# A three-part transformer kernel on one core: the differential bias is written a head ahead, latent outputs get a bank of their own, and neighbourhood heads run in pairs with their score products side by side

## The reference

```python
def diff_attention(q, k, v, lam, subln_w, lam_init):      # 8 heads, 2 maps of 64 each, v of 128
    def block(args):                                      # 16 meta queries, then 4 blocks of 128
        dist = (qpos[:, None] - kpos[None, :]).astype(jnp.float32)
        logits = (jnp.einsum('bhmqd,bhmkd->bhmqk', qblk, kt) * scale
                  - slopes[:, None, None, None] * dist)   # slope of the head: the bias
        probs = jax.nn.softmax(jnp.where(valid, logits, NEG_INF), axis=-1)
        attn = probs[:, :, 0] - lam * probs[:, :, 1]
        return jnp.einsum('bhqk,bhkv->bhqv', attn.astype(vt.dtype), vt)

def _neighbourhood_attention(q, k, v, k_ctx, v_ctx, rpb, n_rows):
    s_loc = jnp.einsum('bjqhd,bjakhd->bhjqak', q_r, k_b) + bias   # keys of the window, with bias
    s_ctx = jnp.einsum('bjqhd,bkhd->bhjqk', q_r, k_ctx)           # and 256 context keys
    p = jax.nn.softmax(jnp.concatenate([s_loc, s_ctx], axis=-1), axis=-1)
    o = einsum(p_loc, v_b) + einsum(p[..., n_loc:], v_ctx)

def _attend(q, k, v):                                     # latent attention: 768 keys, q of 96, v of 64
    s = jnp.einsum('bqhd,bkhd->bhqk', q * q.shape[-1] ** -0.5, k).astype(jnp.float32)
    p = jax.nn.softmax(s, axis=-1).astype(v.dtype)
    return jnp.einsum('bhqk,bkhd->bqhd', p, v)
```

## Time and profile before

| | us |
|---|---|
| median of 3 runs | 3075.2 (3074.88 to 3077.19) |
| the profiled execution's own time | 3074.74 |
| its span, first to last instruction | 3072.9 |
| TensorE busy | 2920.8 (95%) |
| VectorE busy | 1528.0 (50%) |
| ScalarE busy | 1144.4 (37%) |
| GpSimd busy | 35.1 (1%) |
| TensorE clock granted, mean | 0.969 |

### The profile page before, as it was taken

One profiled execution on the slowest core, in us unless ns is written; L12 is line 12 of the kernel. 1 busy time (PEld: TensorE's weight loads), 2 busy tenths in 40 slices (PEclk: granted clock), 3 DMA queues, 4 the chain that ended last, 5 costly groups with the idle time before them and its releaser, 6 DMA issues.

```text
span 3072.9 us, 42976 instructions
## 1 busy us (share of the span) xinstructions
PE 2920.8 (95%) x14922; PEld 2397.4 (78%) x14922; DVE 1528.0 (50%) x2441; ACT 1144.4 (37%) x1767; POOL 35.1 (1%) x28
## 2 busy tenths in 40 slices
PE   8999998899999999999999999889889899899998
PEld 6878777679987888879988888867656677788887
DVE  3335444455565666667744654655443434433334
ACT  4333355432223233255532423523444443432223
POOL 0000000000000000000000000000000000000000
PEclk9999999899999999999999999899889999899999
DMA  3224211143443554546643333311111113133332
GB/s 115 69 68 134 66 48 52 58 132 114 124 130 98 163 153 151 155 123 173 180 117 94 89 96 91 107 42 33 42 32 37 35 33 99 56 89 90 95 96 82
DMA packets 504093, 288.73 MB, mean 94 GB/s; under 512 B 17577, under 2 KB 483962, under 8 KB 503850
## 3 DMA queue, kind: packets, MB, share of 16 engines
q1 hardware_dynamic: 503978, 287.25, 31.9%
HBM read 285.12 MB, written 2.10 MB: 93 GB/s over the span
## 4 chain that ended last, share of the span: by engine, by line
PE 68%; issue 20%; DVE 5%; ACT 4%; DVEq 1%; ACTq 1%; DMA 0%; POOL 0%; POOLq 0%; SPq 0%
PE unit_acc L789 61%; DVE w_lo L2030 2%; PE aux L773 1%; PE aux L1340 1%; ACT w_hi L1439 1%; PE aux L1225 1%; PE aux L1316 1%; PE aux L916 1%; DVE mla_stat L2763 1%; PE aux L1207 1%; PE aux L810 1%; PE aux L1208 0%; ACT mla_p L1931 0%; DVE mla_pT L2769 0%; DVEq L2034 0%
## 5 line engine op out<-in xcount | busy, mean ns | idle before, releaser
L789 PE MATMUL unit_acc<-h_hi,w_hi 128*128 128x512 f32 (+1 forms) x2376 | 839.1, 377 | 21.7 <-DVE w_lo L2030 11.2
L789 PE MATMUL unit_acc<-h_lo,w_hi 128*128 128x512 f32 (+1 forms) x2376 | 816.7, 368 | 0.0
L789 PE MATMUL unit_acc<-h_hi,w_lo 128*128 128x512 f32 (+1 forms) x2376 | 815.2, 367 | 0.0
L2030 DVE TENSOR_TENSOR w_lo<-raw,w_hi 128x1024 fp32r<-128x1024 f32 (+3 forms) x418 | 496.6, 1188 | 578.5 <-ACT w_hi L1439 571.7
L1439 ACT ACTIVATE w_hi<-raw 128x1024 fp32r<-128x1024 f32 (+3 forms) x418 | 430.4, 1030 | 698.3 <-PE unit_acc L789 654.2
L789 PEld LDWEIGHTS unit_acc<-h_hi,w_hi 128*128 128x128 f32 x2376 | 431.5, 192 | 120.9 <-issue 21.4
L789 PEld LDWEIGHTS unit_acc<-h_hi,w_lo 128*128 128x128 f32 x2376 | 430.8, 191 | 78.3
L789 PEld LDWEIGHTS unit_acc<-h_lo,w_hi 128*128 128x128 f32 x2376 | 433.0, 192 | 72.1
L789 PE MATMUL unit_acc<-branch_hi,w_hi 128*128 128x512 f32 x448 | 178.3, 398 | 0.1
L789 PE MATMUL unit_acc<-branch_hi,w_lo 128*128 128x512 f32 x448 | 177.6, 397 | 0.0
L789 PE MATMUL unit_acc<-branch_lo,w_hi 128*128 128x512 f32 x448 | 177.6, 396 | 0.0
(11 more groups left out here) (368 smaller groups left out, 3696.1 us busy)
## 6 DMA issues: line engine op xcount, KB each, us to landing
raw<-in_ffn_w_dram SPq DMA_DIRECT2D x180, 512.0 KB, 3.8
raw<-in_w_in_dram SPq DMA_DIRECT2D x142, 512.0 KB, 3.9
ada_raw<-in_w_ada_dram SPq DMA_DIRECT2D x72, 512.0 KB, 4.7
raw<-in_w_up_dram SPq DMA_DIRECT2D x32, 512.0 KB, 4.2
raw<-in_w_down_dram SPq DMA_DIRECT2D x32, 512.0 KB, 3.9
raw<-in_w_branch_dram SPq DMA_DIRECT2D x24, 512.0 KB, 3.9
raw<-in_ffn_w_dram SPq DMA_DIRECT2D x24, 384.0 KB, 3.4
raw<-in_w_out_dram SPq DMA_DIRECT2D x16, 512.0 KB, 3.9
```

Of the source, the lines that this page charges most:

```text
L789: last = pe.matmul(G[s][0:n, 512 * j:512 * j + m], w[:, k, 0:n], x[:, k, a:a + m], start=(k == 0 and i == 0), stop=(k == kc - 1 and i == 2))
L2030: dve.tensor_tensor(wl[s][:, 0:kc, :], raw[s][:, 0:kc, :], wh[s][:, 0:kc, :].bitcast(F32), ALU.subtract).then_inc(lo_split, 1)
```

## The change

What it does, by place:

- The context's sum of squares stands after unit 7 of the feed-forward part, not after unit 6.
- Differential heads: ScalarE writes `diff_bias` for the next head after the last exponents of this one (`head_bias`), and for head 0 ahead of the loop. The filler is cut 4 and 4 chunks instead of 3 and 5, ScalarE copies the transposes of tile 4 before it takes the next head's projection, and VectorE's weight splits stand elsewhere.
- The start of the neighbourhood stage: splits stand between the three tables, and units 0 to 2 run one after another.
- Neighbourhood pairs: 4 steps, each of both heads. The four score products alternate between rows 0 to 63 and 64 to 127 of the array and write one bank for each head. Both heads share statistics instructions of two columns; one copy by ScalarE moves all eight transposes (VectorE's two copies before), ScalarE copies the values too, and the value products of both heads go to `NA_OUT`, a bank of `G[0]`.
- Latent heads: the value product goes to `MLA_OUT`, the second bank of one of the two accumulators, and waits for its own tile's copies alone; transposes no longer wait for the output before. Filler and splits are cut anew, a drain is added ahead of the reciprocal.

The diff, cut to what moves work:

```diff
+        NA_OUT = G[0][:, 512:512 + P]
+        MLA_OUT = G[Count(U_MLA).slot][:, 512:512 + VD]
...
                 qk(4)
-                fill(0, 0, 3)
+                fill(0, 0, 4)
                 qk(3)
...
-                fill(0, 3, 8)
+                fill(0, 4, 8)
...
-                    if final and n == 6:
+                    if final and n == 7:
                         sum_squares(ssc, GC)
...
+                def qk(t):
                     a = NA_START[t]
-                    pe.matmul(A[0][:, b:b + 256], q, nk[r, a:a + 256], start=True, stop=True)
-                    pe.matmul(A[0][:, b + 256:b + 512], q, kct[r, 2 * i + p, :], start=True, stop=True).then_inc(n_qk, 1)
+                    for b, k, k0 in ((0, nk, a), (256, kct[:, 2 * i + p, :], 0)):
+                        for e in range(2):
+                            r = slice(64 * e, 64 * e + 64)
+                            last = pe.matmul(A[0][:, 512 * e + b:512 * e + b + 256], nq[r, P * t:P * t + P],
+                                             k[r, k0:k0 + 256], start=True, stop=True)
+                    last.then_inc(n_qk, 1)
...
+                def pv(t):
+                    pe.wait_ge(n_at, val(at_(t + 1)))
+                    pe.wait_ge(n_o, val(at_(t) + 1))
...
-            for c in range(KC):
-                for k in range(2):
-                    unit(Count(U_NA + k), H2H, H2L, GS, ready=None if k else (ap_lo, 5 * KC),
-                         part=(c, c + 1))
-            unit(Count(U_NA + 2), H2H, H2L, GS)
+            for k in range(3):
+                unit(Count(U_NA + k), H2H, H2L, GS, ready=None if k else (ap_lo, 5 * KC))
...
                     if t:
                         pe.wait_ge(k_ad, val(cnt(t)))
                         pe.wait_ge(k_at, val(cnt(t)))
-                    if t > 1:
-                        pe.wait_ge(k_o, val(cnt(t - 1)))
...
-                    pe.wait_ge(k_ad, val(cnt(min(t + 2, NT))))
+                    pe.wait_ge(k_ad, val(cnt(t + 1)))
+                    if t:
+                        pe.wait_ge(k_o, val(cnt(t)))
                     for j in range(6):
-                        last = pe.matmul(A[1][:, 768:768 + VD], mT[t % 2][:, j, :], mV[:, j, :],
+                        last = pe.matmul(MLA_OUT, mT[t % 2][:, j, :], mV[:, j, :],
...
+            def head_bias(head):
+
+                act.activation(dR[:, :], rel[:, :], ACT.Copy,
+                               scale=cst("slope8")[:, bass.ds(head, 1)]).then_inc(d_bias, 1)
...
                 exps(3)
+                copy_pT(4)
                 next_head(0)
-                copy_pT(4)
                 exps(2)
                 out_o(4)
                 copy_pT(3)
                 exps(1)
+                if more:
+                    head_bias(head + 1)
                 out_o(3)
                 copy_pT(2)
...
+                    act.wait_ge(n_tr, val(turn(i, t + 1 + NT * p, 2 * NT)))
+                    act.activation(nT[:, :, :, :], A[1][:, :].rearrange("p (e c n) -> p e c n", e=2, n=P),
+                                   ACT.Copy).then_inc(n_at, 1)
...
                 for t in (4, 3, 2, 1):
                     logits(t)
+                    if t == 4:
+                        split(u + 4)
                     combine(t)
-                    if more and t == 3:
+                    if more and t == 2:
                         split(u + 5)
...
+                if kind < 2:
+                    split(Count(U_NA + kind + 2))
...
                 for t in range(NT):
                     if t < NT - 1:
                         row_max(t + 1)
+                    if more and t == 1:
+                        split(u + 2)
+                    if more and t == 2:
+                        split(u + 3, 4)
                     copy_pT(t)
                     if t:
                         out_o(t - 1)
-                    if more and t == 0:
-                        split(u + 2)
-                    if more and t == 1:
-                        split(u + 3, 4)
```

More of the change, by code:

```diff
@@ L1210, in transpose_p, with at_ @@
[L1210 to L1215, removed]
-                    last.then_inc(n_tr, 1)
[L1218 to L1222, removed]
-                    v0 = NA_START[t] // 64
-                    for j, v in enumerate((v0, v0 + 2, NV, NV + 1)):
-                        last = pe.matmul(A[1][:, 512:512 + NA_HD], nT[s % 2][:, j, :], nV[:, v, 64 * e:64 * e + 64],
-                                         start=(j == 0), stop=(j == 3))
+                def at_(t):
+                    return turn(i, t + NT * p, 2 * NT)
@@ new lines, in pv @@
+                def pv(t):
+                    pe.wait_ge(n_at, val(at_(t + 1)))
+                    pe.wait_ge(n_o, val(at_(t) + 1))
+                    v0 = NA_START[t] // 64
+                    for e in range(2):
+                        for j, v in enumerate((v0, v0 + 2, NV, NV + 1)):
+                            last = pe.matmul(NA_OUT[:, 64 * e:64 * e + 64], nT[:, e, j, :],
+                                             nV[:, v, 64 * e:64 * e + 64],
+                                             start=(e == 0 and j == 0), stop=(e == 1 and j == 3))
@@ L1599, in diff_head @@
                 head = i * 2 + e
-                act.drain()
-                act.activation(dR[:, :], rel[:, :], ACT.Copy,
-                               scale=cst("slope8")[:, bass.ds(head, 1)]).then_inc(d_bias, 1)
                 exps(4)
@@ L1627, in _ @@
             act.wait_ge(rel_in, 16)
+            head_bias(0)
             for k in range(3):
@@ L2317, in diff_head @@
                                          op1=ALU.subtract).then_inc(br_lo, 1)
-                if more:
-                    split(u + 7)
             dve.drain()
-            for k in range(3):
+            for k in range(2):
                 split(Count(U_DIFF + 2 + k))
@@ L2633, in _, with cnt, logits @@
                         [P, NA_H, 32, GRID_H]), ALU.add)
+                if kind < 2:
+                    split(Count(U_NA + kind + 2))
+            table.then_inc(n_tab, 1)
+            dve.memset(nst[:, :, :], 0.0)
             dve.drain()
-            dve.memset(nst[:, :, :], 0.0).then_inc(n_tab, 1)
-            dve.drain()
-            for k in range(3):
-                split(Count(U_NA + k + 2))
             def na_pair(i, p):
                 u = turn(i, U_NA + 3 * p, 6)
-                for half in range(2):
-                    dve.drain()
-                    dve.wait_ge(n_vt, val(turn(i, half + 1 + 2 * p, 4)))
-                    if half == 0:
-                        dve.tensor_copy(nV[:, 0:5, :], A[1][:, 0:640].rearrange("p (c n) -> p c n", n=P)).then_inc(
-                            n_v, 1)
-                    else:
-                        dve.tensor_copy(nV[:, 5:9, :], A[1][:, 0:512].rearrange("p (c n) -> p c n", n=P)).then_inc(
-                            n_v, 1)
-                def cnt(k):
-                    return turn(i, k + 8 * p, 16)
-                def logits(s):
-                    e, t = divmod(s, NT)
-                    b = s % 2
+                def cnt(t):
+                    return turn(i, t + NT * p, 2 * NT)
+                def logits(t):
                     kind = (0, 1, 1, 2)[t]
@@ L2689, in na_pair @@
-                logits(0)
-                logits(1)
-                for s in range(8):
-                    copy_pT(s)
-                    if s:
-                        out_o(s - 1)
-                    if s < 6:
-                        logits(s + 2)
-                    if s in (3, 6):
-                        split(u + 4 + s // 3)
-                out_o(7)
-                split(u + 7)
+                    dve.wait_ge(n_pv, val(cnt(t + 1)))
+                    at_ = i * 256 + 2 * p * NA_HD
@@ new lines, in out_o @@
+                    dve.tensor_tensor(nO[:, t, at_:at_ + P].rearrange("p (e n) -> p e n", e=2),
+                                      NA_OUT.rearrange("p (e n) -> p e n", e=2),
+                                      nst[:, 7, :].unsqueeze(2).to_broadcast([P, 2, NA_HD]), ALU.mult).then_inc(n_o, 1)
+                logits(0)
+                split(u + 4)
+                for t in range(NT):
+                    reciprocals(t)
+                    if t < NT - 1:
+                        logits(t + 1)
+                    out_o(t)
+                    if t == 1:
+                        split(u + 5)
@@ L2701, in na_pair @@
+                split(u + 6)
                 dve.drain()
@@ L2706, in _ @@
                     na_pair(i, p)
+            split(Count(U_LORA + 4))
             for c in range(4):
```

143 lines of the change are left out of this document (77 added, 66 removed).

## The result

The changed kernel takes 2971.1 us (median, 2969.6 to 2977.4) against 3076.2 for the one before in the same comparison: ratio 0.9661, 95% interval 0.9644 to 0.9678. That is 105 us less, where 90 were forecast. The part on the prediction says where the 15 us come from.

What follows compares the result with a forecast made beforehand. TensorE's own work and its gaps bound the kernel (busy 2920.8 of 3072.9 us). Gains 5.9 + 14.5 + 7.0 + 33.9 + 28.2 = 89.5 took 3074.7 to 2985.2, median 2986 us; 8-in-10 range 2970 to 3012.

Steps and rivals of the forecast that it cites:

- The sum of squares: Context's sum of squares behind unit 7: unit 7 fills the gap of a 4.58 us wait, gaining 5.9 us.
- Differential heads: Score product's 2.65 us wait goes, a new one of about 1.5 us comes at value product 2: 14.5 us gained.
- Start of the neighbourhood stage: Splits between the bias tables end TensorE's 5.17 us wait, a wait of some 0.2 stays: 7.0 us gained.
- Neighbourhood pairs: Eight score records in alternating halves take 1.25 us, idle and low clock shrink in four pairs: 33.9 us gained.
- Latent heads: Output in another bank ends the value product's wait; idle 21.5 to about 2, clock 10.7 to 2: 28.2 us.
- A: Neighbourhood pairs: halves don't overlap, or the chain is longer than the filler; 13.9 us more, 3000 us; chance 0.12.
- B: Pairs, latent and differential heads: the clock doesn't come back, 18 us likely not gained, 3004 us; chance 0.17.
- C: Latent and differential heads: waits only move, the 15.5 us turn up at the transposes, 3001 us; chance 0.13.
- D: Neighbourhood pairs: slower, the level stays at 1.2 GHz through all four, 3120 us; chance 0.03.

Runs made afterwards that it cites:

- the experiment on the bias: The changed kernel with the differential bias written in its own head again, ahead of the exponents of tile 4: 2979.1 us.
- the two kernels above: The kernel before with the latent heads' part alone, 3036.0 us, and the kernel before with the differential part alone, 3059.5 us.
- the kernel with the later bias: The changed kernel with the next head's differential bias written after the transposed copy of tile 1, not ahead of the output of tile 3: 2968.1 us.

## Why the prediction was right, and where it was off

The mechanisms came as written: the waits that were named went, and the new one came where it was expected. The gain came out larger than forecast in each stage, most of all in the latent heads. Heads are counted from 0 here.

*The sum of squares.* 5.9 forecast, 6.3 measured. The wait on the low weights before unit 7 and no wait at the sum, as worked out:

```profile
1293.38 0.50 PE L791 MATMUL unit_acc<-h_hi,w_hi 128*128 128x512 f32 x1 [0.94 <-DVE w_lo L2056]
1299.08 0.60 PE L803 MATMUL aux<-ctx_ssq,const 128*128 128x256 f32 x2
```

*Differential heads.* 14.5 forecast, 14.7 and 17.8 measured. In head 2, which starts at 401.39 here, against the earlier trace rows:

```profile
405.55 0.94 PE L954 MATMUL aux<-diff_k,diff_q 64*128 64x400 f32 x4
...
422.23 1.12 PE L981 MATMUL aux<-diff_v,diff_pT 128*128 128x128 f32 x6 [0.90 <-ACT diff_pT L1603]
```

The 2.65 us wait is gone and the new one is where the queue on ScalarE put it. It is 0.7 to 1.3 us, seven times, 6.8 in all, not 7 x 1.5 = 10.5. Against that, 4.9 us of the old waits stayed and not 2.2: 2.9 at the last head's score products and 2.0 at its value products, which the prediction didn't count. So 13.2 us of waits went where 12.2 were forecast. The clock over the stage rose from 0.93 to 0.94 and 0.95, some 3 and 6 us, where 2.3 were forecast. That the sum agrees with the first profile to 0.2 us is in part luck: errors of 3.7 and 2.7 us nearly cancel. The prediction also read head 2 as typical; as the experiment on the bias shows, the weight split was last in the others.

*Start of the neighbourhood stage.* 7.0 forecast, 8.0 measured; the two kernels above that leave this part as it was took 641.8 and 642.1 us here for 638.9, so the gain may be up to 3 us more. The 5.17 us wait is gone. What stayed is not 0.2: a wait of 2.3 us at the units in turn went (first row, kernel before) and one of 2.0, for another operand, came with the units one after another (second row, changed kernel).

```profile
1992.91 0.71 PE L789 MATMUL unit_acc<-h_hi,w_hi 128*128 128x512 f32 x1 [2.27 <-DVE w_lo L2030]
...
1976.22 0.51 PE L791 MATMUL unit_acc<-h_hi,w_hi 128*128 128x512 f32 x1 [2.01 <-DVE h_lo L2459]
```

The clock was 0.89 over the last 40.6 us ahead of the pairs and is 1.00 over the last 30.9.

*Neighbourhood pairs.* 33.9 forecast, 36.2 measured. A step, against the earlier trace rows:

```profile
2033.57 1.06 PE L775 MATMUL aux<-const,na_p 128*128 128x128 f32 x8 [0.76 <-ACT na_p L1894]
2034.57 0.70 PE L1206 MATMUL aux<-na_k,na_q 64*128 64x256 f32 x4
2035.10 0.60 PE L1206 MATMUL aux<-ctx_k,na_q 64*128 64x256 f32 x4
2035.63 0.50 PE L791 MATMUL unit_acc<-h_hi,w_hi 128*128 128x512 f32 x1
...
2037.14 1.89 PE L1225 MATMUL unit_acc<-na_v,na_pT 128*128 128x64 f32 x16
2040.33 1.04 PE L775 MATMUL aux<-const,na_p 128*128 128x128 f32 x8
```

Idle of 0.8 in a pair and 2.0 in the first came as written. Eight records took 1.06 (2034.57 to 2035.63), not 1.25: the Trainium skill's rule ("TensorE: Matmul & The Clock Gate", Part 3) was the better of the two values, by 3 us in the sum. Low clock cost 1.4 us, not 3.

*Latent heads.* 28.2 forecast, 33.6 and 35.2 measured; this is the term that was mis-sized. The prediction took "235.5 us of work" as busy time less slow clock, and let only the shown idle go. But busy time itself fell: 232.3 less 0.01 x 234 is 230.0. The 5.5 us between them are the part of a wait that the rows count as busy. The value product of tile 0 started 2.50 us after its transposes (2313.10 here, and 2315.60 in the earlier trace rows) where it now takes 0.66, so its wait cost 1.84, 0.16 more than the 1.68 shown. The next two rows are tile 1:

```profile
2313.10 0.82 PE L773 MATMUL aux<-const,mla_p 128*128 128x128 f32 x6
...
2322.03 0.82 PE L773 MATMUL aux<-const,mla_p 128*128 128x128 f32 x6
2323.02 1.52 PE L1340 MATMUL aux<-mla_v,mla_pT 128*128 128x64 f32 x12 [0.17 <-DVE mla_pT L2769]
```

It is 0.99 from start to start there, of which 0.17 is shown: again 0.16 more than shown. If the eight waits of the score product are like them, 32 waits in the stage make 5.1. The terms for idle (2) and clock (2) were right: 1.8, and 0.01 x 234 = 2.3.

*Rivals.* A (no overlap) is out: it took a chunk in between to bring it about. B (the clock doesn't come back) is out for the pairs, by 0.91 to 0.99, and for the latent heads, by 0.96 to 0.99, though pauses of 0.8 us stayed in three pairs; in the differential heads only a part came back. C (the waits only move) is out: the latent 15.5 us turned up nowhere, and the 6.8 at value product 2 are less than half of the 16.8 that the differential score product no longer waits. D is out.

The stages' gains add up to 98.8 us in the first profile and 103.7 in the second; less the 1.7 at the end that is 97 and 102, as the spans have it (97.3 and 102.5). The forecast of 89.5 is short of them by 8 and 13, and the latent heads alone make 5.4 and 7.0 of that. The 105 of the medians is 3 more than the second; the runs of the kernel before scatter by 7 to 14 us in each comparison of the experiments, and what of it is chance stays open.

## What to carry to other kernels

A wait cost more than its row showed here, as the products ahead of it no longer overlapped with the one behind: read the distance from start to start with and without the wait, in every head and not in one. When an instruction is moved off one chain, follow the queue that it now stands in: there it will be late next. A shorter chain can pay twice, since a slow clock can follow the pause: all four waits of 2.06 us in the pairs of the kernel before were followed by a low stretch in its profile. But compare low clock over several executions before counting it as a gain of an edit.

## What the runs showed of the hardware

- Two products of 64 rows in different halves of the array run at the same time even when they aren't neighbours in the program: 1.07 us for eight records in either order, 2 x 1.06 = 2.12 with three full-height products between them. With both products of one half first in the program, the first of the other half still started within 0.3 us of the group's start (two records in the first 0.49).
- A wait between the transposes and the product that needs their copy cost 0.16 us more than its gap: 2.50 against 0.66 with 1.68 shown, 0.99 with 0.17 shown, and 0.94 with a gap of 0.12 that the view doesn't print.
- The same wait of 1.3 us in the same place was followed by a granted clock of 0.68 over 10.6 us in one execution and of 1.00 in the next (the two rows shown with the result). The same wait of 2.04 us at the first pair's transposes was followed by low clock in the changed kernel (0.99 over the pairs) and by none in the kernel with the later bias (1.00). What decides between them the runs don't show.
